# The first tile of an expert layer in turns of two entries, diagonals ahead of copies, and four places for gather indices

## The reference, cut to what matters

```python
def peer(x, w_pq, subkeys, pu, pv):
    qp = (x @ w_pq).reshape(T, PEER_HEADS, 2, D_PKEY // 2)
    s = jnp.einsum('thcd,hcnd->thcn', qp, subkeys).astype(f32)
    s1, i1 = lax.top_k(s[:, :, 0], PEER_TOPK)
    s2, i2 = lax.top_k(s[:, :, 1], PEER_TOPK)
    cand = (s1[..., :, None] + s2[..., None, :]).reshape(...)
    ...
    top_s, sel = lax.top_k(cand, PEER_TOPK)
    eidx = jnp.take_along_axis(cidx, sel, axis=-1)
    g = jax.nn.softmax(top_s, axis=-1)
    u = pu[eidx]
    vv = pv[eidx]
    a = jax.nn.gelu(jnp.einsum('thkd,td->thk', u, x).astype(f32))
    return jnp.einsum('thk,thkd->td', (g * a).astype(vv.dtype), vv)
```

## Time and profile before

| | |
|---|---|
| three runs, median | 1319.68 us (1317.98 to 1320.13) |
| the profiled execution's own time | 1318.5 us |
| its span, first to last instruction | 1316.7 us |
| mean granted TensorE clock | 0.971 |
| busy in the span: PE, DVE, POOL, ACT | 1126.7, 802.9, 707.7, 448.5 us |
| moved by DMA | 459.12 MB, of it 402.68 by the gathers |

### The profile page before, as it was taken

One profiled execution on the slowest core, in us unless ns is written; L12 is line 12 of the kernel. 1 busy time (PEld: TensorE's weight loads), 2 busy tenths in 40 slices (PEclk: granted clock), 3 DMA queues, 4 the chain that ended last, 5 costly groups with the idle time before them and its releaser, 6 DMA issues.

```text
span 1316.7 us, 12818 instructions
## 1 busy us (share of the span) xinstructions
PE 1126.7 (86%) x3320; PEld 548.5 (42%) x3320; DVE 802.9 (61%) x1865; ACT 448.5 (34%) x1348; POOL 707.7 (54%) x898
## 2 busy tenths in 40 slices
PE   6999999999997899889878786888887888788786
PEld 4655666576443455545423332332223222222222
DVE  4356414579769644775887888854556455455554
ACT  2012213213333333233353342534434434434433
POOL 1000000305666555555678685677777787787760
PEclk9999999999998999999989898899998999999999
DMA  9655414059999899989999999999999999999995
GB/s 343 149 161 213 158 64 144 16 207 412 410 392 399 331 416 367 335 335 351 425 424 425 426 426 425 424 426 426 427 425 426 426 425 427 426 426 426 426 426 234
DMA packets 70175, 459.12 MB, mean 349 GB/s; under 512 B 7428, under 2 KB 15976, under 8 KB 18160
## 3 DMA queue, kind: packets, MB, share of 16 engines
q0 software_dynamic: 55296, 402.68, 74.3%
q1 hardware_dynamic: 13984, 55.17, 11.9%
q10 hardware_dynamic: 848, 0.71, 0.2%
HBM read 450.82 MB, written 7.71 MB: 348 GB/s over the span
## 4 chain that ended last, share of the span: by engine, by line
PE 39%; DMA 32%; POOL 10%; DVE 9%; issue 5%; ACT 4%; POOLq 0%; ACTq 0%; DVEq 0%
DMA arena<-in_peer_uv,arena 31%; PE ps L1206 14%; PE ps L897 8%; PE ps L903 5%; PE ps L1194 4%; POOL arena L630 4%; DVE arena L1666 3%; POOL arena L629 2%; ACT arena L820 2%; POOL arena L606 1%; POOL arena L623 1%; PE ps L1117 1%; ACT arena L814 1%; POOL arena L605 1%; ACT arena L681 1%
## 5 line engine op out<-in xcount | busy, mean ns | idle before, releaser
L1206 PE MATMUL ps<-arena 128*128 128x512 f32 x1536 | 738.0, 623 | 165.7 <-ACT arena L820 165.7
L1666 DVE CUSTOM_DVE_ANT_0 arena<-arena 128x1024 f32<-128x1024 f32 x384 | 467.9, 1233 | 342.5 <-DMA arena<-in_peer_uv,arena 341.1
L1206 PEld LDWEIGHTS ps<-arena 128*128 128x128 f32 x1536 | 283.9, 196 | 605.7 <-ACT arena L820 316.6
L630 POOL DMA_INDIRECT arena<-in_peer_uv,arena x256 | 300.3, 1173 | 55.1 <-issue 48.9
L812 ACT ACTIVATE arena<-arena 128x1 f32<-128x1 f32 x384 | 76.8, 200 | 410.5 <-DVE arena L1666 409.8
L606 POOL DMA_INDIRECT arena<-in_peer_uv,arena x128 | 153.2, 1197 | 27.5 <-issue 21.3
L820 ACT ACTIVATE arena<-arena 128x128 f32<-128x128 f32 x384 | 154.2, 402 | 20.1
L681 ACT ACTIVATE arena<-ps 128x512 f32<-128x512 f32 (+2 forms) x63 | 30.6, 510 | 292.7 <-PE ps L1194 128.5
L814 ACT ACTIVATE arena<-arena 128x1 f32<-128x1 f32 (+1 forms) x384 | 113.1, 294 | 29.9
L629 POOL TENSOR_TENSOR arena<-arena 128x1 f32<-128x1 f32 x256 | 110.4, 431 | 15.1 <-POOL arena L623 9.2
L897 PE MATMUL ps<-arena 128*128 128x384 f32 (+1 forms) x336 | 111.1, 487 | 0.0
(11 more groups left out here) (234 smaller groups left out, 744.1 us busy)
## 6 DMA issues: line engine op xcount, KB each, us to landing
arena<-in_w_in SPq DMA_DIRECT2D x8, 2048.0 KB, 10.0
arena<-in_w_pq SPq DMA_DIRECT2D x6, 2048.0 KB, 9.7
arena<-in_peer_uv,arena POOLq DMA_INDIRECT x384, 27.0
arena<-in_w_out SPq DMA_DIRECT2D x4, 1024.0 KB, 6.2
arena<-in_state_C SPq DMA_DIRECT2D x1, 2064.0 KB, 7.5
out_new_C_s<-arena SPq DMA_DIRECT2D x1, 2064.0 KB, 6.9
arena<-in_cache_k SPq DMA_DIRECT2D x4, 512.0 KB, 11.4
arena<-in_cache_v SPq DMA_DIRECT2D x1, 2048.0 KB, 11.7
```

The source lines that it names most:

```text
L630: nc.gpsimd.indirect_dma_start(slots[HALF * g + s], None, d["peer_uv"], bass.IndirectOffsetOnAxis(ap=isl[g][:, s:s + 1], axis=0)).then_inc ...
L1206: last = mm(ps[:, BANKS + half, :], diag[:, s, :], slots[SLOTS * h + s][:, DM + 512 * half:DM + 512 * half + 512], start=first and s == 0, ...
L1666: v.tensor_tensor_reduce(slots[k][:, 0:DM], slots[k][:, 0:DM], hn[t], 1.0, 0.0, ALU.mult, ALU.add, aslot[:, s:s + 1]).then_inc(a_ok, 1)
```

## The change

The first tile goes in 64 turns (`PIECES`) of two entries (`PIECE`) instead of 32 half rounds of four.

- TensorE: a half of `y` is cut into four parts of two matmuls in successive turns, a `qq` block into two parts of four matmuls. `sc22` and `sc23` come first.
- ScalarE: the two entries' gelus, weights and diagonals now come ahead of the copies of `hnT` and `qq` of the same turn; a `qq` is copied in the turn of its second part.
- VectorE: `subkeys` for one head of a block at a time, `pairs` for one head at a time, `experts` for groups of two heads (`PARTS` has 11 groups instead of 8), the norm cut into squares and scales of one tile each. The routing of block 1 of tile 2 moves from ahead of the loop into its first two turns. Tile 1's routing stays in larger pieces, in 12 late steps instead of 8.
- GpSimd: even and odd rounds have index places of their own (`isl[0..1]` and `isl[2..3]`), and the copy into one waits for the diagonals of two rounds back. The loop over rounds is written out. At the second tile's start there is a wait on `diag_ok` ahead of the copies into `isl[2]` and `isl[3]`.

```diff
-LATE = 8
+LATE = 12
+PIECE = 2
+PIECES = HK // PIECE
-PARTS = [(2, 0, 1, 0), (2, 1, 1, 1), (2, 2, 2, 2), (2, 4, 4, 4), (0, 4, 4, 0), (0, 0, 4, 4), (1, 4, 4, 0), (1, 0, 4, 4)]
+PARTS = [(2, 0, 1, 0), (2, 1, 1, 1), (2, 2, 2, 2), (2, 4, 2, 4), (2, 6, 2, 6),
+         (0, 4, 2, 0), (0, 6, 2, 2), (0, 2, 2, 4), (0, 0, 2, 6), (1, 4, 4, 0), (1, 0, 4, 4)]
...
 def query_steps():
-    steps += [[("qq", i)] for i in (8, 9, 10, 11)]
+    for i in (8, 9, 10, 11, 12, 13, 14, 15, 4, 5, 6, 7, 0, 1, 2, 3):
+        for part in range(2):
+            steps[at] += [("qq", i, part)]
+            at += 1
...
 def routing_steps():
+    put(34, *sub(a, 2), *pairs(a, 4, 5), *experts(5))
...
-            def gather(n, t, i, first):
+            def gather(n, t, i, odd, first):
+                done = i * SLOTS
                 for g in range(2):
+                    k = 2 * odd + g
                     if not first:
-                        pool.wait_ge(diag_ok, done * SLOTS - SLOTS + HALF * g + HALF)
-                    nc.gpsimd.tensor_copy(isl[g], ...)
+                        pool.wait_ge(diag_ok, done - 2 * SLOTS + HALF * g + HALF)
+                    nc.gpsimd.tensor_copy(isl[k], ...)
...
             def gather_wide(n, t, i, first):
                     else:
+                        pool.wait_ge(diag_ok, done - SLOTS + HALF * (g - 2) + HALF)
                         filled(pool, plan[-1][0])
...
@@ scalar
-                    for i in range(ROUNDS):
-                        for g in range(2):
-                            for what, *k in query_steps()[2 * i + g]:
-                                (copies of hnT and qq)
-                            weights_of(i * SLOTS, n, t, i * SLOTS, range(HALF * g, HALF * g + HALF))
-                            step_exps(2 * i + g)
+                    for q in range(PIECES):
+                        i, s = divmod(q * PIECE, SLOTS)
+                        weights_of(i * SLOTS, n, t, i * SLOTS, range(s, s + PIECE))
+                        for what, *k in query_steps()[q]:
+                            (copies of hnT, and of qq in its second part)
+                        step_exps(q)
...
@@ tensor
-                g = i % 2
-                weigh(0, i // 2, i < 2, i // 2 == ROUNDS - 1, 0, range(HALF * g, HALF * g + HALF))
+                i, s = divmod(q * PIECE, SLOTS)
+                weigh(0, i, i == 0, i == ROUNDS - 1, 0, range(s, s + PIECE))
...
@@ vector
-            route_subkeys(2, 1)
             steps = routing_steps()
-            for i in range(2 * ROUNDS):
-                dots(0, ORDER[0], i // 2, 0, range(HALF * g, HALF * g + HALF))
-                for step in steps[i]:
+            for q in range(PIECES):
+                dots(0, ORDER[0], i, 0, range(s, s + PIECE))
+                for step in steps[q]:
                     take_step(*step)
```

More of the change, by code:

```diff
@@ L141, in query_steps @@
-    steps += [[("sc", a, 0)], [("sc", b, 2)], [("sc", b, 3)], [("sc", b, 1)], [("sc", b, 0)]]
-    return steps + [[]] * (2 * ROUNDS - len(steps))
+    steps = [[] for _ in range(PIECES)]
+    steps[0] += [("sc", 2, 2)]
+    steps[1] += [("sc", 2, 3)]
+    at = 2
+    for t in (a, b):
+        for i in range(2):
+            for part in range(4):
+                steps[at] += [("y", t, i, part)]
+                at += 1
+    for t in (a, b):
+        steps[22] += [("hnT", t, i) for i in range(2)]
@@ L155, in routing_steps, with put, sub @@
-    late = [[("subkeys", b, 2)], [("subkeys", b, 3)], [("pairs", b, 4), ("pairs", b, 6)], [("experts", 6, 0), ("experts", 6, 1)],
-            [("subkeys", b, 1)], [("subkeys", b, 0)], [("pairs", b, 0), ("pairs", b, 2)], [("experts", 7, 0), ("experts", 7, 1)]]
-    assert len(steps) == 2 * ROUNDS and len(late) == LATE
+    steps = [[] for _ in range(PIECES)]
+    def put(q, *what):
+        for w in what:
+            steps[q].append(w)
+            q += 1
+    def sub(t, i):
+        return [("subkeys", t, i, (0,)), ("subkeys", t, i, (1,))]
@@ new lines, in pairs, with experts @@
+    def pairs(t, *heads):
+        return [("pairs", t, h, 1) for h in heads]
+    def experts(part):
+        return [("experts", part, 0), ("experts", part, 1)]
+    put(0, *sub(2, 1), *pairs(2, 2, 3), *experts(2), *sub(2, 2), *sub(2, 3))
+    put(10, ("y", a, 0), ("y", a, 1), *pairs(2, 4, 5), *experts(3), ("y", b, 0), *pairs(2, 6, 7))
+    put(11, ("square", a))
+    put(19, ("y", b, 1), ("scale", a), ("scale", b))
+    put(19, ("square", b))
+    put(22, *experts(4))
+    put(34, *sub(a, 2), *pairs(a, 4, 5), *experts(5))
@@ L158, in routing_steps @@
+    put(42, *sub(a, 3), *pairs(a, 6, 7), *experts(6))
+    put(50, *sub(a, 1), *pairs(a, 2, 3), *experts(7))
+    put(58, *sub(a, 0), *pairs(a, 0, 1), *experts(8))
+    late = [[("subkeys", b, i, (0, 1))] for i in (2, 3)] + [[("pairs", b, h, 2)] for h in (4, 6)] + [[x] for x in experts(9)]
+    late += [[("subkeys", b, i, (0, 1))] for i in (1, 0)] + [[("pairs", b, h, 2)] for h in (0, 2)] + [[x] for x in experts(10)]
+    assert len(late) == LATE
     return steps + late
@@ L634, in _ @@
             for n, t in enumerate(ORDER):
-                for part, (u, head, heads, pos) in enumerate(PARTS):
+                for part, (u, _, heads, pos) in enumerate(PARTS):
                     if u != t:
```

139 lines of the change are left out of this document (71 added, 68 removed).

## The result

| | before | changed |
|---|---|---|
| runs, median | 1319.59 us (4 runs, 1317.98 to 1320.13) | 1287.45 us (4 runs, 1286.57 to 1290.24) |
| ratio to before, 95% interval | | 0.9757 (0.9737 to 0.9776) |
| span of the profiled execution | 1316.7 us | 1284.8 us |
| mean granted TensorE clock | 0.971 | 0.969 |

The change makes the kernel 32.1 us faster. The forecast was 1294 in a range of 1286 to 1308, a gain of 25.5.

What follows compares the result with a forecast made beforehand. TensorE and a bubble were taken to bound the first tile's query blocks, transfers the rest. A gain of 26.5, less 3 for unevenness, plus 2 elsewhere, made 25.5 us: from 1319.68 to 1294, range 1286 to 1308.

Steps and rivals of the forecast that it cites:

- What bounds the kernel: First tile: TensorE and a bubble bound the query blocks' part, transfers the rest; 39 us of idle transfers at most to gain.
- The query stretch: First tile's sixteen query blocks: four entries take 10.31 us instead of 11.91, the part 168.5 instead of 195.05, 26.5 less.
- Less 3 for unevenness: Query blocks' part of the first tile: 3 us of the gain lost, with three engines at 97, 86 and 100%.
- First and last stretch +2: First tile before and after the query blocks: a gain of 2 us, between -3 and +6.9.
- The sum: Whole kernel: 26.5 less 3 plus 2 gives 25.5 us, the span falling from 1316.7 to 1291.2.
- The second and third tile last as long as before: Later tiles: transfers already booked fully at 426 GB/s, a rate the edit does not touch, so no change.
- The second index place: GpSimd's index copy: refills up to 2 us earlier, no gain by itself, but keeps the DMA queue deep enough for 97%.
- Exponentials: ScalarE, first tile: six more table loads, 7.7 us, covered by turns without query copy; uncovered, 2.8 us each would show.
- Transfers fuller than their bytes: Rival, query blocks' part: DMA share 0.93 is the true load, so at most 14.8 us to gain, 1305; chance 0.18.
- GpSimd as the limit: Rival, first tile: GpSimd cannot issue gathers faster, only 3 us gained, 1316, or no change; chance 0.05 together with the staying bubble.
- VectorE as the limit: Rival, first tile: cutting VectorE's pieces saves nothing, so VectorE becomes the bound and time rises to 1338; chance 0.03.
- The bubble stays: Rival, query blocks: ScalarE reaches its copy late, period stays 11.91, 1318; chance 0.05 together with GpSimd's issue limit.

Runs made afterwards that it cites:

- the second multiply: The changed kernel with one more small multiply on GpSimd ahead of each of the first tile's 128 gathers: 1288.15 us.
- the blocks spread: The changed kernel with its 16 query blocks over turns 24 to 61, every sixth turn free, and the last routing moved into the second tile: 1289.53 us.
- the load experiment: The changed kernel with an unused 128x1024 multiply added on VectorE in every second query turn, 1289.5 us, or in every one, 1300.49 us.

## Why the prediction was right, point by point

**What bounds the kernel: right.** TensorE and a bubble in the query stretch, the transfers elsewhere. The earlier trace rows gave 32 us of idle transfers there, and 28 of them came back.

**The query stretch: right in the mechanism and the period, lucky in the last microsecond.** The period was 10.31 in the sum and 10.32 measured. The length was 168.5 in the sum and 168.49 measured, but the sum has four score blocks in it and the stretch only three, at 483.70, 526.57 and 568.75; the fourth comes at 607.47, behind it. With three the sum is 167.6. The 0.9 us that make up for it are 0.2 of rounding in the period and 0.7 in four turns between 495 and 527, which last 5.26 to 5.49 us instead of 5.16 (a score block not counted); the weight loads' 2.4 us of waiting for diagonals are the only wait in the rows that fits. The switches between kinds of matmul are free, as the first stretch had said. A slip of reading did no harm: the eight matmuls of 6.87 us in the earlier trace rows are one half of an output projection, not two. And the sixteen periods of 11.91 left 4.4 of the 195.05 us without an owner; they are the two pauses behind exponentials and the slow matmuls, 4.6 us, which the new order took away as well. The copy is covered in both kernels with the new order, and comes into the open in the one without it.

**"Less 3 for unevenness": wrong.** It was next to nothing, the 0.7 us above. The reason given was three engines at 97, 86 and 100%, and the 86% for VectorE is where it failed. The prices were right, but 36.3 us for every 16 entries puts four groups of routing into the stretch, and it holds three: 64 x 1.15 + 3 x (4 x 2.87 + 6.38) = 127.2 us, against 127.68 measured, which is 76%. The 97% for the transfers was about right: 416 GB/s is 98%, 70.1 MB instead of the 69.4 of the same stretch before.

**"First and last stretch +2": mis-sized.** In idle transfers they gave (5.8 - 0.6) + (1.1 - 0.4) = 5.9, near the upper end of 6.9. The experiments say where from: whole VectorE pieces lose 5.0, whole blocks on TensorE 3.5 and the single index place 1.3 (within the spread), with 22.7 for the order. These come to 32.5 against 32.1, but they were measured from different ends and overlap, so the agreement proves little. The cutting of `y` and `qq` was costed at nothing on TensorE, which holds; that it also gives something, by freeing slots more evenly where the transfers bound, was missing from the sum. So was the norm's wait of 3.19 us as a term of its own; it is gone, and lies inside the 5.9.

**The sum.** 28.0 + 5.9 = 33.9 us of idle transfers gone, 2.0 of it not seen in the span; 25.5 had been forecast. Of the 36.4 us by which TensorE ended the first tile earlier (640.24 against 676.60) 4.5 were given back: the part behind it is 644.56 long instead of 640.10. Before:

```profile
676.60:1316.70 640.10, 503.37 (x1024) 186.10 (x1024) 385.51 (x779) 254.29 (x791) 455.58 (x560) 0.96 0.99 416
```

Between the first windows and the last ones the later tiles run at 425 to 426 GB/s in both. By the rates the part behind the mark has 18.2 us of idle transfers in the changed kernel and 15.0 before, with an uncertainty of some 0.8 in each from the rounding of the rate. Of the difference, 0.4 stands at the start (421 GB/s to 680) and 2.6 at the end, where the last 44.8 us carry 260 GB/s and the last 40.7 before carried 270. The rest is what was left to move, 0.5 MB more or 1.2 us, which is no more than the rounding. Why the end is longer stays open. "The second and third tile last as long as before" is thus true of the transfers' rate, and 4.5 us off when counted from TensorE's mark. The two mis-sized terms were both too cautious, and this one took part of it back.

**The second index place: right.** Nothing beyond the spread by itself, from both sides. That it keeps the queue deep is not shown: with one place the changed kernel is no slower by more than its spread. The wait that was added for the new places cost nothing, as forecast; their first copies in the second tile (644.23 and 653.35) stood for no diagonals. But the copy ahead of them, at 627.43, stood 4.1 us for diagonals of the last round, though its place was last read a round earlier and its slot was free at 623.1, behind the first entry of 621.34. The transfers run at 412 GB/s from 630 to 640. Whether a looser wait would give anything was not tried.

**Exponentials: right, with a condition.** They are covered in the new order. Without it the prediction put 2.8 us on each. The old order shows 3.1 in three places, but made up otherwise: 1.43 of pause, since one of the two table loads (at 518.41) is hidden behind the query block, and 1.70 from TensorE's clock, which the prediction had no term for.

**The rivals.** Transfers fuller than their bytes: refuted, a share of 1.01 at 416 GB/s, and 424 in single windows. The DMA share of 0.93 before was thus no measure of what was to be had; the bytes were. GpSimd as the limit: refuted by the second multiply. The Trainium skill ("SBUF — State Buffer", Who interferes with whom) says that a VectorE instruction with two SBUF inputs contends with a GpSimd instruction that reads SBUF. The traces agree, row by row (last section), and with the multiply on VectorE in every query turn the mean issue from 308 to 640 rose from 1188 to 1247 ns. It doesn't matter here, since GpSimd has the time: one issue takes 963 to 1916 ns, against 963 to 1979 before. VectorE as the limit: exists, but some 20 us of evenly spread work away. *The bubble stays:* refuted, as ScalarE's wait for query matmuls and TensorE's for diagonals show.

## What to carry to other kernels

In an engine that works in order, a copy that must wait for a long block of its consumer stands in front of the small work that the same consumer needs next; put the small work first, and look for this wherever engine A waits for B with a long total and B waits for A with a short one of the same count. In a stretch where one engine is the limit, its rows back to back give the new period to a hundredth, if one counts what lies in the stretch and not what lies in a typical part of it. A finer cut of the work paid here where the transfers were the limit and moved nothing in TensorE's own rows. And an average over a stretch can say that added work fits where a group of turns says that it doesn't, as the load on VectorE did, so work is summed by group. Count a gain in idle transfer time (bytes over the flat rate), not by a mark on one engine or by the DMA share: in the table above it gives the change in span within 2.1 us in eleven of twelve profiles, and it says in which window the time was lost.

## What was not expected of the hardware

**TensorE's clock after short pauses.** Ahead of the first query block TensorE has pauses, at diagonals and then about 3.2 us at the copies of `hnT`. In the profiled execution of the changed kernel the granted clock stayed at 1.00 behind them. In that of the kernel with whole blocks, and in others, it did not. TensorE in order of time in the kernel with whole blocks, then a window of it (columns of the window as above):

```profile
431.17 9.94 PE L1254 MATMUL ps<-arena 128*128 128x512 f32 x16 [3.17 <-ACT arena L724]
```

```profile
430.00:435.00 5.00, 3.83 (x5) 1.76 (x6) 4.86 (x11) 4.88 (x10) 0.00 (x0) 0.50 1.00 424
```

The same sixteen records take 9.94 us instead of 7.52, at 0.50, the lower of its two levels (1.2 of 2.4 GHz); the changed kernel had 1.00 in this window. It was also 0.50 in this window with one index place, and 0.69 to 0.74 with the blocks spread, with whole VectorE pieces and with the second multiply, so it doesn't follow one edit. Shorter pauses can do it: in the changed kernel with copies first, all three pauses of 2.75 us were followed by slow matmuls (1.70 us each), and of the two in the kernel before the second was (585.05, 8.83 instead of 7.13) and the first not (440.67, 7.13). Where TensorE is the limit this is lost time. Where the transfers are, it isn't shown that it reaches the end: with one index place, at 0.50 in this window too, the span is 1286.4 us against 1284.8.

**DMA share.** A share of 1.00 stood beside 405 GB/s (540 to 580, changed kernel), one of 1.01 beside 412 (580 to 620) and beside 424 (420 to 460). So a share of 1 doesn't say that the rate was reached.

**When a gather's issue is long.** An issue that starts while a dot product runs on VectorE (1.23 us, two inputs in memory) is long, and one that starts just ahead of it is not. Two rows of the kernel before, where dot products started at 494.04 and 496.75:

```profile
494.31 1.79 POOL L606 DMA_INDIRECT arena<-in_peer_uv,arena  x1 [0.15 <-issue]
...
496.60 0.97 POOL L606 DMA_INDIRECT arena<-in_peer_uv,arena  x1
```

In the changed kernel, of 120 issues from 310 to 640, the 29 that started with 0.75 to 1.25 us of a dot product still to run took 1.61 to 1.92 us, the 3 that started with it 0.97 to 0.98, and the 41 beside an idle VectorE 0.96 to 1.11. Beside the small searches of the routing, 0.3 to 0.4 us long, they took 0.96 to 0.98. Five that started during the added multiply of the load experiment (two inputs) took 1.63 to 1.81.

**GpSimd's records.** With 48.7 us of small multiplies more, the indirect DMAs beside them are shorter in the records (mean 1188 ns to 1068), and the multiply in front longer (437 to 488). The cause stays open.
